# One slot fewer for weight loads, one slot more for split weight pieces, in a transformer block pair on one core

## The reference

```python
x = x + 0.5 * mod[:, 0, 2] * swiglu(modulate(x, ...), ffn_w13[l, 0], ffn_w2[l, 0])
y = hybrid_mixer(modulate(x, ...), cos, sin, w_in[l], ...)
x = x + mod[:, 1, 2] * y
x = x + 0.5 * mod[:, 2, 2] * swiglu(modulate(x, ...), ffn_w13[l, 1], ffn_w2[l, 1])
```

## Time and profile before

| | |
|---|---|
| median of three runs | 1066.14 us |
| profiled execution: own time | 1066.5 us |
| profiled execution: span | 1064.5 us |
| TensorE busy | 1027.7 us, 97% |
| VectorE busy | 700.2 us, 66% |
| ScalarE busy | 537.3 us, 50% |
| bytes read | 209.88 MB |

### The profile page before, as it was taken

One profiled execution on the slowest core, in us unless ns is written; L12 is line 12 of the kernel. 1 busy time (PEld: TensorE's weight loads), 2 busy tenths in 40 slices (PEclk: granted clock), 3 DMA queues, 4 the chain that ended last, 5 costly groups with the idle time before them and its releaser, 6 DMA issues.

```text
span 1064.5 us, 19831 instructions
## 1 busy us (share of the span) xinstructions
PE 1027.7 (97%) x8502; PEld 994.4 (93%) x8502; DVE 700.2 (66%) x1213; ACT 537.3 (50%) x903; POOL 39.0 (4%) x75
## 2 busy tenths in 40 slices
PE   5999999999988999999999999999999999999995
PEld 4899999988987899999999999999999999999985
DVE  3478886557687577776656778655457775555485
ACT  4453543455554655544444577554355554444453
POOL 5000000010000001000000000003000000000000
PEclk7999999999999999999999999999999999999998
DMA  9979889876734445577655456336156575565511
GB/s 304 380 251 318 310 319 322 287 247 204 212 109 159 157 144 155 197 244 271 205 191 183 135 178 218 120 123 175 60 163 216 187 237 164 194 198 163 195 40 40
DMA packets 144463, 212.27 MB, mean 199 GB/s; under 512 B 4259, under 2 KB 121239, under 8 KB 144376
## 3 DMA queue, kind: packets, MB, share of 16 engines
q1 hardware_dynamic: 138928, 194.40, 54.9%
q0 software_dynamic: 5184, 16.30, 4.8%
q10 hardware_dynamic: 264, 0.31, 0.1%
HBM read 209.88 MB, written 1.11 MB: 198 GB/s over the span
## 4 chain that ended last, share of the span: by engine, by line
PE 67%; issue 22%; DVE 7%; ACT 2%; DMA 1%; SPq 0%; POOL 0%; POOLq 0%; DVEq 0%; ACTq 0%
PE PS L460 65%; DVE wlo L1769 4%; PE PS L468 2%; DMA SC<-in_w_ada_dram 1%; ACT whi L1286 1%; DVE SC L1727 1%; DVE xT L1736 0%; DVE W L1727 0%; DVE hl L1736 0%; ACT SC L1278 0%; DVE st L1739 0%; DVE SC L1733 0%; DVE SS L1727 0%; ACT SC L1273 0%; DVE SC L2202 0%
## 5 line engine op out<-in xcount | busy, mean ns | idle before, releaser
L1769 DVE TENSOR_TENSOR wlo<-raw,whi 128x1024 fp32r<-128x1024 f32 (+2 forms) x331 | 386.8, 1186 | 203.2 <-ACT whi L1286 202.6
L1286 ACT ACTIVATE whi<-raw 128x1024 fp32r<-128x1024 f32 (+2 forms) x331 | 331.9, 1022 | 176.7 <-PE PS L460 137.7
L460 PE MATMUL PS<-hh,whi 128*128 128x256 f32 (+1 forms) x1376 | 393.8, 286 | 6.8 <-DVE wlo L1769 4.6
L460 PE MATMUL PS<-hh,wlo 128*128 128x256 f32 (+1 forms) x1376 | 388.6, 282 | 0.0
L460 PE MATMUL PS<-hl,whi 128*128 128x256 f32 (+1 forms) x1376 | 387.9, 282 | 0.0
L460 PE MATMUL PS<-SR,whi 128*128 128x256 f32 (+1 forms) x1824 | 329.1, 283 | 4.0 <-DVE wlo L1769 1.4
L460 PEld LDWEIGHTS PS<-SR,whi 128*128 128x128 f32 x1824 | 279.8, 188 | 8.9 <-issue 2.6
L460 PEld LDWEIGHTS PS<-hh,whi 128*128 128x128 f32 x1376 | 260.2, 189 | 12.8 <-DVE wlo L1769 6.5
L460 PEld LDWEIGHTS PS<-hl,whi 128*128 128x128 f32 x1376 | 261.0, 190 | 0.4
L460 PEld LDWEIGHTS PS<-hh,wlo 128*128 128x128 f32 x1376 | 260.8, 190 | 0.0
L460 PE MATMUL PS<-SR,wlo 128*128 128x256 f32 (+1 forms) x912 | 256.7, 281 | 0.0
(11 more groups left out here) (183 smaller groups left out, 714.5 us busy)
## 6 DMA issues: line engine op xcount, KB each, us to landing
raw<-in_ffn_w_dram SPq DMA_DIRECT2D x60, 1024.0 KB, 7.2
raw<-in_w_in_dram SPq DMA_DIRECT2D x38, 1024.0 KB, 5.4
raw<-in_w_ff_dram SPq DMA_DIRECT2D x32, 1024.0 KB, 5.3
raw<-in_w_ada_dram SPq DMA_DIRECT2D x16, 1024.0 KB, 6.6
SC<-in_w_ada_dram POOLq DMA_DIRECT2D x12, 1024.0 KB, 6.4
SC<-in_w_ada_dram SPq DMA_DIRECT2D x8, 1024.0 KB, 12.2
raw<-in_w_out_dram SPq DMA_DIRECT2D x8, 1024.0 KB, 4.9
raw<-in_ffn_w_dram SPq DMA_DIRECT2D x8, 768.0 KB, 12.6
```

What stands on the lines that cost most here:

```text
L460: return e.matmul(o, l, r, start=start, stop=stop, skip_group_check=True)
L1286: e.activation(hi_part(p), raw_part(p), ACT.Copy).then_inc(*hi_done.up(p.i))
L1769: e.tensor_tensor(lo_part(p), raw_part(p), hi32(hi_part(p)), ALU.subtract).then_inc(*lo_done.up(p.i))
```

## The change

The ring of loads has three slots of 8 KB a partition in place of four, and each of the two rings of split pieces has seven slots of 4 KB in place of six; the memory taken, 80 KB a partition, is the same.

```diff
-NRAW = 4
-NP = 6
+NRAW = 3
+NP = 7
```

## The result

Four runs of the changed kernel took 1073.31 to 1075.73 us, median 1074.99, against 1066.16 for the kernel before: a ratio of 1.0081 with a 95% interval of 1.0064 to 1.0099. It is 8.8 us slower, where +3.6 was forecast, and 0.8 us above the top of the range. The direction and the two largest terms (attention and the last gate) were right; the ring of loads in the first feed-forward network costs several times what I gave it.

A forecast was written before the change was run, and what follows sets the result against it. TensorE's in-order work was taken as the bound, so the rings act only through its pauses. Terms -1.2 + 5.6 + 1.0 - 2.3 + 0.5 = +3.6 gave a median of 1069.7 us, range 1063.6 to 1074.2.

The forecast's parts named there:

- part 5: First feed-forward network, 82 to 162 us: three load slots cost one small pause, +0.5 us, bounds 0 and +5.
- part 1: Gates, 243 us: a seventh slot lets piece 73 be split earlier, -1.2 us, bounds 0 and -1.4.
- part 3: Clock behind the attention pause: half rate for 3.4 us of work, +1.0 us kept, bounds 0 and +2.5.
- Part 2: Start of attention, 306 to 329 us: late load 62 holds up ScalarE's copies, +5.6 us, ends -1.7 and +7.4.
- Part 4: Last gate, 1027 us: piece 324's low part made earlier, shorter pause and less clock loss, -2.3 us, bounds 0 and -2.8.
- my sign of being wrong: First feed-forward network: forecast wrong if TensorE waits for low parts more than 2 us together before 165 us.
- What I gave nothing: Everywhere else: TensorE's lead over loads is 7 us or more, one slot less costs 2 to 4 of it, so nothing.
- B: Rival, first feed-forward network: load circle runs at 19 us or above, +3 to +5 more, 1073 to 1074.5; chance 0.2.
- the forecast: The whole kernel slower, likeliest 1069.7 us, own range 1068.3 to 1071.5; chance 0.43.
- A: Rival at attention: load 62 is not waited for, only gains are left, 1061 to 1062 us; chance 0.13.
- C: Rival at attention: delay only 2 to 4 us, cancelled by the gains, no change, 1064.2 to 1068.2; chance 0.24.

The follow-up runs named there:

- places6: Kernel before, rings unchanged (four load, six piece slots), several split parts moved to other places at gates, attention and the last gate: 1057.45 us, ratio 0.9920.
- lo94early: Changed kernel with low parts of pieces 93 and 94 moved ahead of VectorE's copies of the second half's transposes: 1070.34 us, ratio 1.0028.
- hold99: Changed kernel with the high part of piece 99 moved behind ScalarE's two transpose copies and the convolution copy: 1069.06 us, ratio 1.0022.
- r3p6: Kernel before with three load slots in place of four, rings of pieces kept at six: 1079.37 us, ratio 1.0126.
- places7b: Changed kernel with the moves of hold99 and lo94early, plus one low part instead of four ahead of attention's first score minimum: 1065.46 us, ratio 0.9994.
- places6r3: The kernel of places6 with three slots for loads in place of four, nothing else: 1067.88 us, ratio 1.0015 against the kernel before.
- copyfirst: Changed kernel with ScalarE's rounded copy of each hidden tile in the first feed-forward network put ahead of the following high parts: 1086.50 us, ratio 1.0192.
- places7: Changed kernel with the moves of hold99, lo94early and copyfirst, plus one low part instead of four ahead of attention's first score minimum: 1077.17 us, ratio 1.0097.
- adaspread: Changed kernel with the first feed-forward network's modulation loads spread 1, 1, 1, 2, 2, 2, 2, 1 over its eight later steps: 1074.39 us, ratio 1.0077.

## Why the prediction was wrong

In the sum, the step that failed is part 5, the first feed-forward network: +0.5, where the stage came out at +3.0 in the change's profile and at +5.2 in the mean of four profiles of the same program. Beside it part 1's gain was eaten, part 3 was too large, and 0.8 us came from a stage that had been put at nothing. The parts in turn:

**Part 1, the gates: half right.** The pause of 1.40 us went (piece 73 is split early), as said. But a pause of 0.95 us for a modulation row at 231 and one of 0.33 at 256 came in its place, so nothing is left of the 1.2 us. The bound of 0 that I gave was the result. places6 has the gain whole: -1.9 for its first stage.

**Part 2, attention: right.** +5.4 for the score minimum against 5.6, with each link in its row. The three links (release, landing, order) are confirmed by lo94early and hold99.

**Part 3, the clock: right in kind, too large in the sum.** From 331 to 339 us the change shows, with columns as in the earlier trace rows,

```profile
331.00:339.00 8.00, 7.16 (x41) 6.93 (x42) 4.92 (x16) 4.87 (x12) 0.00 (x0) 0.68 0.75 249
```

that is 8 x 0.32 x 2 = 5.1 us at the lower level, in place of 3.4. TensorE is 8.4 us late at the pause before head 2 (331.84 against 323.42) and 8.5 at the milestone of 377, although its later pauses in between fell from 2.6 to 0.8 us; so the clock cost about 1.7 us and those waits took up all of it. In the sum that is +0.1, not the +1.0 that I had kept after letting 0.7 vanish: I had written that no slack follows in the next heads, though the kernel before waits 1.20, 1.03 and 0.33 us there. Parts 2 and 3 together are so +5.5, not +6.6. The Trainium skill, which the prediction cites ("TensorE: Matmul & The Clock Gate", section "Part 1: The HAM clock gate (the "warmup" mystery)"), states that the clock falls to its lower level when TensorE has been idle; the row behind this pause agrees.

**Part 4, the last gate: right.** -2.5 against -2.3: 1.98 to 0.90 of pause, and a clock of 1.00 behind it. r3p6 gives the share of each: it keeps the pause (1.99 us) but not the lower clock, and its last stage is -1.5, so the clock is about 1.5 us of the 2.5 and the pause the rest.

**Part 5, the first feed-forward network: this step failed.** I gave it +0.5, with +5 as the bound. The profile after has two pauses there, 1.43 and 0.95 us, 2.4 together, and hold99, lo94early and places7b, which are the same program as the change up to 300 us, have +6.8, +3.7 and +7.2 at the first milestone where the change has +3.0. The mean of the four is 5.2. These are profiles of runs that lay on both sides of their medians; if what parts each of them from its kernel's median is put into this stage, the four give 4.7, 4.1, 4.5 and 4.6 us (an estimate). The stage holds part 1 too, whose gain and whose new pauses cancel. Three things were wrong:
- The arithmetic. By the prediction's numbers as they stand, three steps of 17.5 to 18.5 us take 1.8 to 4.8 us from a lead of 8.2 and leave 3.4 to 6.4, not 0.4 to 3; and three of 18.5 to 20 overdraw it by 1.1 us at most, not 5. So neither +0.5 nor its bound followed from the working.
- The lead. I took 8.2 us at 124 us, read from a kernel with four slots, and counted three steps from 106. A count of pieces at one moment is also more than TensorE has at the worst piece: in the kernel before, low part 39 is made at 127.2 us and TensorE comes to it at 132.4, 5.2 us later. The ring of three is a circle from its first `ada` step on: high part 27, which needs the second up load, starts at 93.5 us in place of 91.9, then the up loads of the change land at 111.5, 129.7 and 149.8, steps of 18.0, 18.2 and 20.1 us. My 17.5 to 18.5 was right for two of three, but the lead was already down when the count began: the low part of 30 is finished 2.3 us before TensorE takes it, 5.2 in the kernel before. The steps of 18.0, 18.2 and 20.1 us are together 5.6 over three times 16.9, and by the third nothing is left: low part 45 is made at 152.1, when TensorE has waited 0.95 us for it.
- What waits. I asked only when TensorE would miss a piece. At 111 us it misses the product of the hidden tile, behind ScalarE's high part in the same queue. The longest of these pauses, 3.42 us in hold99, also drops the clock (0.62 from 112 to 120 us). So my sign of being wrong, over 2 us of waits for low parts before 165 us, stayed silent in the changed kernel (0.95 us) while the term failed.

**What I gave nothing:** the same blocking by a load in the second network (ScalarE waits 1.16 us for a load before its high part of 444.36 us, and its rounded copy stands behind it), 1.02 us of TensorE at 448 us. Every kernel here with three slots has it, 0.99 to 1.14 us; places6 and the kernel before, with four, have not. The middle stage of places6 is +0.9 all the same, in small parts that I have not traced to a cause.

**The 2 us between the profiled execution (+6.8) and the medians (+8.8).** The changed kernel's profile is its fastest run, and its first stage is the smallest of the four profiles of that program, 2.2 us under their mean. Kernels with three slots also tend to spread more: the sets of 12 runs (hold99, lo94early, places7b, places6r3) lie within 5.0 to 6.3 us, the two sets of 23 of the kernel before within 4.1 and 4.7. That the change's other runs lost their 2 us in this stage is likely by this and not shown: they have no trace.

**The rivals.** B had the mechanism and the place, and gave 1073 to 1074.5, close to the result. Its threshold of 19.6 us for a step was passed by one step of three only, and the mean was 18.8: with the true lead of some 5 us the threshold is 16.9 + 5.2/3 = 18.6, and I should have let B and the forecast share one distribution. A and C hung on load 62 being early, which it was not.

## What to carry to other kernels

A ring's depth is worth what stands between two uses of a slot: before one is taken away, write the lap (landing, split, release, issue, landing) beside the consumer's time for the same work, from the first step at which the lap is closed, and not with a lead read where the ring was deeper. Then ask of each in-order engine what stands behind the instruction that will wait for a load, for that is what gets late, rather than the piece itself. And if a deeper ring seems to gain by shifting the order, first try the order alone: here it gave 8.6 us with no memory moved.

## What the runs showed of the hardware

One pause does not always do the same to the clock. After 1.98 us of idle time at 1027 us in the kernel before, the granted clock was 0.66 in the mean of the next five microseconds; after 1.99 us at the same place of the program in r3p6 it stayed at 1.00:

```profile
1042.00:1047.00 5.00, 4.32 (x36) 4.35 (x37) 5.00 (x6) 2.39 (x4) 0.00 (x0) 1.00 0.66 208
```

The thirteen profiles have more such pairs. The pause at the first milestone is 1.72 to 1.74 us long in twelve of them; in the 5 us behind it the clock is at 1.00 in ten and at 0.66 in copyfirst and places7. Of five pauses of 1.97 to 2.04 us two are followed by 0.66 (the kernel before, places7) and three by 1.00 (r3p6, adaspread, copyfirst). Behind all fifteen pauses of 2.25 us and more after the first 60 us it is at 0.50 to 0.68. Behind 1.43 us (the change, 111 us) and 1.08 us (places7b) it stays at 1.00. So a gain that rests on a clock drop behind a pause of about 2 us, as part of my part 4 did, is one that some executions have and others don't. What decides it is not shown here.
